# Two weight blocks multiplied by seven products in place of eight, with the weight sums on GpSimd

## The reference, cut to what matters

```python
for l in range(DEPTH):                    # second_block, two layers
    h = rmsnorm(x, norm_g[l])             # 256 x 1024
    p = h @ w_in[l]
    (c_q, c_kv, k_r, gate_a, fq, fk, fv, ff, gate_b,
     shift_cols, gate_c, merge_cols) = split_cols(p, IN_SIZES)
    o_a = mla_branch(..., gate_a, ...)    # attention, times silu(gate_a)
    o_b = fox_branch(..., gate_b, ...)    # attention with decay, times silu(gate_b)
    o_c = rwkv_branch(..., gate_c, ...)   # recurrence, times silu(gate_c)
    g_a, g_b, g_c = jnp.split(merge_cols, 3, axis=-1)
    merged = (jax.nn.sigmoid(g_a) * (o_a @ w_pa[l]) + jax.nn.sigmoid(g_b) * (o_b @ w_pb[l])
              + jax.nn.sigmoid(g_c) * (o_c @ w_pc[l]))
    x = x + merged @ w_out[l]
```

## Time and profile before

| | us |
|---|---|
| median of 3 runs | 2013.91 (2013.78 to 2015.64) |
| the profiled execution | 2013.13 |
| its span, first to last instruction | 2011.3 |
| TensorE busy in the span | 1642.2 |
| VectorE busy | 575.9 |
| ScalarE busy | 336.2 |
| GpSimd busy | 144.8 |
| fill products (L1662), 768 records | 188.1 |

### The profile page before, as it was taken

How to read it: one execution, slowest core, us unless ns; L and a number is a source line. 1 busy time by engine, 2 the same in 40 slices (tenths; PEclk the granted TensorE clock), 3 DMA queues, 4 the chain that set the end, 5 groups by cost and what they waited for, 6 DMA issues and landing times.

```text
span 2011.3 us, 25746 instructions
## 1 busy us (share of the span) xinstructions
PE 1642.2 (82%) x11426; PEld 940.9 (47%) x11426; DVE 575.9 (29%) x1055; ACT 336.2 (17%) x725; POOL 144.8 (7%) x137
## 2 busy tenths in 40 slices
PE   6988865655657998665657559999999999999999
PEld 3544221111214863111212118887668687775785
DVE  0546010000105652100100013542433625533435
ACT  1141100000000001000000001342332013433320
POOL 0000000000000001000000000211021302110213
PEclk8998888887877998787887888999999999999999
DMA  9998999999999979999999993321532342214330
GB/s 403 415 394 318 426 427 428 428 428 428 428 428 427 426 280 411 423 428 427 428 428 428 428 428 115 127 78 33 212 146 97 118 175 83 85 45 185 147 114 33
DMA packets 45741, 588.67 MB, mean 293 GB/s; under 512 B 5184, under 2 KB 5344, under 8 KB 9920
## 3 DMA queue, kind: packets, MB, share of 16 engines
q1 hardware_dynamic: 42624, 575.05, 69.2%
q0 software_dynamic: 2576, 10.54, 1.3%
q10 hardware_dynamic: 432, 1.44, 0.2%
HBM read 585.96 MB, written 1.06 MB: 292 GB/s over the span
## 4 chain that ended last, share of the span: by engine, by line
PE 57%; DMA 38%; DVE 3%; ACT 2%; issue 1%; SPq 0%; ACTq 0%; DVEq 0%
DMA arena<-in_experts 37%; PE ps L1281 17%; PE ps L1662 8%; PE ps L1549 5%; PE ps L1685 4%; PE ps L1681 4%; PE ps L1454 3%; PE ps L2032 2%; DMA ring<-in_stream 1%; PE ps L1783 1%; PE ps L2062 1%; PE ps L2105 1%; PE ps L1245 1%; PE ps L1770 1%; PE ps L1561 1%
## 5 line engine op out<-in xcount | busy, mean ns | idle before, releaser
L1549 PE MATMUL ps<-arena 128*32 128x512 f32 x1372 | 218.9, 763 | 137.7 <-DMA arena<-in_experts 136.1
L1549 PE MATMUL ps<-ring,arena 128*32 128x512 f32 x1312 | 207.8, 763 | 117.1 <-DMA ring<-in_experts 114.3
L1281 PE MATMUL ps<-arena,ring 128*128 128x256 f32 (+1 forms) x992 | 192.2, 357 | 2.5 <-ACT arena L773 2.5
L1662 PE MATMUL ps<-arena,ring 128*128 128x256 f32 x768 | 188.1, 389 | 0.2 <-issue 0.2
L1281 PEld LDWEIGHTS ps<-arena,ring 128*128 128x128 f32 x992 | 171.1, 195 | 23.1 <-ACT arena L773 3.1
L1549 PEld LDWEIGHTS ps<-arena 128*32 128x32 f32 x1372 | 44.8, 125 | 277.5 <-DMA arena<-in_experts 150.8
L1549 PEld LDWEIGHTS ps<-ring,arena 128*32 128x32 f32 x1312 | 41.5, 126 | 252.6 <-DMA ring<-in_experts 139.7
L1662 PEld LDWEIGHTS ps<-arena,ring 128*128 128x128 f32 x768 | 139.8, 190 | 29.8 <-issue 10.6
L2482 DVE TENSOR_TENSOR arena<-ps,gate 128x512 f32<-128x512 f32 x16 | 10.3, 686 | 306.2 <-PE ps L1549 306.2
L1681 PE MATMUL ps<-arena,ring 128*128 128x256 f32 x384 | 89.5, 382 | 0.0
L881 ACT ACTIVATE arena<-ps,modcol 128x128 f32<-128x128 f32 x32 | 14.6, 457 | 434.0 <-PE ps L1561 434.0
(11 more groups left out here) (426 smaller groups left out, 2046.8 us busy)
## 6 DMA issues: line engine op xcount, KB each, us to landing
arena<-in_experts SPq DMA_DIRECT2D x85, 2048.0 KB, 40.7
ring<-in_experts SPq DMA_DIRECT2D x82, 2048.0 KB, 40.9
ring<-in_stream SPq DMA_DIRECT2D x59, 2048.0 KB, 8.8
spare<-in_experts SPq DMA_DIRECT2D x21, 2048.0 KB, 40.6
arena<-in_stream SPq DMA_DIRECT2D x13, 2048.0 KB, 20.8
spare<-in_stream SPq DMA_DIRECT2D x3, 2048.0 KB, 19.1
ring<-in_stream SPq DMA_DIRECT2D x2, 1696.0 KB, 7.3
arena<-in_stream SPq DMA_DIRECT2D x2, 1024.0 KB, 26.5
```

What stands on the lines that cost most here:

```text
L1281: mm = M(dst, lhs(k), rhs(k), start=k == 0, stop=k == n - 1)
L1549: mm = M(bank(b + half)[32 * e:32 * e + 32], x[:, k, 32 * e:32 * e + 32], wk(e, half), start=k == 0, stop=k == KD - 1, tile_position=(0, 3 ...
L1662: mm = M(bank(fill_bank(n))[:, x * T:x * T + T], slot(key)[:, k, c:c + P], s2["ht"][:, k], start=k == 0, stop=k == KD - 1)
```

## The change: seven products for eight

Eight of the nine blocks are put together in pairs, so that a pair is a matrix of 1024 x 1024. It is cut into quarters b11, b12, b21, b22 and multiplied by the tokens, which are cut in halves of 128 tokens and of four tiles. Seven products of quarters (16 products of 128 x 128 weights by 128 tokens each) stand in place of eight. Sums of weight quarters are made in place, in the slots, by GpSimd; sums of tokens once per layer by VectorE; ScalarE copies partial results out of PSUM and VectorE adds them. Three pairs are the whole fill of the recurrence, the fourth stands in the attention. A step of the filler is now two products of half the width. The order of the weights in the stream changes: gate_b goes behind the merge blocks of gate a, and latent behind the first half of merge gate b.

In the diff `pair_out` is a function of ScalarE's program, `product` and the seven lines behind it are TensorE's, `pair_in` and `filled` VectorE's, `decays`, `pair_differences`, `pair_updates` and the last `second` GpSimd's. ScalarE's and VectorE's parts are called at fixed points of their programs, each when the fill up to that point holds the product that it needs.

```diff
-FILLS = {(0, 0): dict(FILL, open=6, down=0, lora=5, kk_sum=15, rk_sum=8, gn_sum=27),
-         (1, 0): dict(FILL, open=4, down=2, lora=11, kk_sum=14, rk_sum=8, gn_sum=22),
-         (0, 1): dict(FILL, open=0, down=0, lora=6, kk_sum=15, rk_sum=8, gn_sum=32)}
+FILLS = {(0, 0): dict(FILL, open=6, down=0, lora=5, kk_sum=15, rk_sum=8, gn_mean=7, gn_sum=14),
+         (1, 0): dict(FILL, open=4, down=2, lora=9, kk_sum=14, rk_sum=8, gn_sum=14),
+         (0, 1): dict(FILL, open=0, down=0, lora=6, kk_sum=15, rk_sum=8, gn_mean=6, gn_sum=16)}
-ATT_FILL = (6, 0) + (6, 5) * 6 + (6, 6) * 2
+ATT_FILL = (6, 0) + (5, 5) * 6 + (6, 5) * 2
+PAIRS = ((("gate_c",), ("gate_a",)), (("merge", 0, 0), ("merge", 0, 1)), (("gate_b",), ("merge", 1, 0)),
+         (("merge", 2, 0), ("merge", 2, 1)))
+WOVEN = 3
+PRODUCTS = 7
+PRODUCT = 8
+PAIR = PRODUCTS * PRODUCT
+PLAIN = 6
...
-        add(("in", layer, "gate_b"), rows(wi[:, G_B:G_B + HALF]))
...
         merge(0, 0)
         merge(0, 1)
+        add(("in", layer, "gate_b"), rows(wi[:, G_B:G_B + HALF]))
+        merge(1, 0)
         add(("in", layer, "latent"), rows(wi[:, C_Q:G_A]))
-        merge(1, 0)
...
+            def pair_out(l, n, i):
+                if i == 0:
+                    act.wait_ge(*Sp.at(l, n, 0))
+                    if n:
+                        act.wait_ge(*Sv.at(l, n - 1, "sum22"))
+                    A(part_e, bank(7), ACT.Copy).then_inc(*Sa.up(l, n, "e"))
+                if i == 1 and n and n < WOVEN:
+                    pair_last(l, n - 1)
+                if i == 2:
...
+                    A(part_u, bank(7), ACT.Copy).then_inc(*Sa.up(l, n, "u"))
+                if i == 3:
+                    act.wait_ge(*Sv.at(l, n, "sum11"))
+                    pair_gate_out(l, n, 0, 0)
+                if i == 4:
+                    act.wait_ge(*Sp.at(l, n, 4))
+                    act.wait_ge(*Sv.at(l, n, "sum11"))
+                    A(part_e, bank(7), ACT.Copy).then_inc(*Sa.up(l, n, "w"))
...
+                if p:
+                    filled_to(l, pair_ends(1, 4))
...
+                def product(i, b, weights, tokens, fresh):
+                    for tile in range(4):
+                        for k in range(4):
+                            mm = M(bank(b)[:, tile * P:(tile + 1) * P], weights[:, k, tile * P:(tile + 1) * P], tokens[:, k],
+                                   start=fresh and tile == 0 and k == 0, stop=tile == 3 and k == 3, skip_group_check=True)
+                            if tile == 3 and k == 3:
+                                if i < PRODUCTS - 1:
+                                    mm.then_inc(*Sp.up(l, n, i))
+                                else:
+                                    mm.then_inc(used, 3 if n == WOVEN - 1 else 2)
+                            if k % 2:
+                                yield
...
+                yield from product(0, x, b11, ht[:, 0:4, 0:P], True)
...
+                yield from product(1, y, b21, ht[:, 4:8, 0:P], True)
+                pe.wait_ge(*Sa.at(l, n, "e"))
+                pe.wait_ge(*S("token_dve").at(l, 3))
+                pe.wait_ge(*So.at(l, n, "t2"))
+                yield from product(2, x, part_sum, token_sums[:, 1], False)
+                pe.wait_ge(*Sv.at(l, n, "sum11"))
+                pe.wait_ge(*So.at(l, n, "t3"))
+                yield from product(3, y, b11, token_sums[:, 2], True)
+                pe.wait_ge(*Sa.at(l, n, "u"))
+                yield from product(4, x, b12, token_sums[:, 0], False)
+                pe.wait_ge(*Sa.at(l, n, "w"))
+                yield from product(5, x, b22, token_sums[:, 3], False)
+                pe.wait_ge(*Sv.at(l, n, "sum22"))
+                pe.wait_ge(*So.at(l, n, "t4"))
+                yield from product(6, y, b21, ht[:, 4:8, P:T], False)
...
+            def pair_in(l, n, i):
+                if i == 1:
+                    ve.wait_ge(*Sp.at(l, n, 1))
+                    ve.wait_ge(*Sa.at(l, n, "e"))
+                    V.tensor_tensor(pair_quarter(n, 0, 0), by_tile4(bank(6)), by_tile4(part_e), ALU.add).then_inc(*Sv.up(l, n, "sum11"))
+                if i == 4:
...
+                if i == 6:
...
...
                 V.scalar_tensor_tensor(out=rw["kmod"], in0=rw["kmod"], scalar=1.0, in1=k, op0=ALU.add, op1=ALU.mult
                                       ).then_inc(*Sv.up("kmod", *K))
+                filled(3)
...
             def decays(l):
                 for j in range(4):
+                    if j == 2:
+                        pair_differences(l, WOVEN)
+                        pair_updates(l, WOVEN)
                     if j >= 2:
                         po.wait_ge(*Sv.at("score", 1, l, 2 + j))
...
+            def pair_differences(l, n):
+                for key in pair_keys(l, n):
+                    po.wait_ge(*has_landed(key))
+                G.tensor_tensor(b12, b12, b11, ALU.subtract).then_inc(*So.up(l, n, "t1"))
+                po.wait_ge(*So.at(l, n, "t1"))
+                if n:
+                    po.wait_ge(*Sp.at(l, n - 1, 2))
+                    po.wait_ge(*So.at(l, n - 1, "t4"))
+                G.tensor_tensor(part_sum, b22, b12, ALU.subtract).then_inc(*So.up(l, n, "t2"))
+
+            def pair_updates(l, n):
+                po.wait_ge(*So.at(l, n, "t2"))
+                po.wait_ge(*Sp.at(l, n, 0))
+                G.tensor_tensor(b11, part_sum, b11, ALU.subtract).then_inc(*So.up(l, n, "t3"))
+                po.wait_ge(*Sp.at(l, n, 1))
+                G.tensor_tensor(b21, b21, part_sum, ALU.subtract).then_inc(*So.up(l, n, "t4"))
...
             def second(l):
+                pair_differences(l, 0)
+                pair_updates(l, 0)
                 for p in range(2):
...
+                    if p == 0:
+                        pair_differences(l, 1)
+                        pair_updates(l, 1)
+                        pair_differences(l, 2)
+                    else:
+                        pair_updates(l, 2)
```

More of the change, by code:

```diff
@@ L625, in merge_gate @@
             return tab2[:, n_second + i * 2 * T:n_second + (i + 1) * 2 * T].rearrange("p (j t) -> p j t", j=2)
-        def merge_done(l, b, i):
[L629 to L641, removed]
+        part_sum = spare[:, 0:2048].rearrange("p (k n) -> p k n", k=4)
@@ new lines, in two_block_program, with pair_keys, pair_blocks, pair_gate @@
+        part_e = spare[:, 2048:2560]
+        part_u = spare[:, 2560:3072]
+        token_sums = ln_t[:, :].rearrange("p (i k t) -> p i k t", i=4, k=4)
+        def pair_keys(l, n):
+            return tuple(("in", l) + part for part in PAIRS[n])
+        def pair_blocks(l, n):
+            first, second_ = (slot(key) for key in pair_keys(l, n))
+            return first[:, 0:4], second_[:, 0:4], first[:, 4:8], second_[:, 4:8]
+        def pair_gate(n, j):
+            part = PAIRS[n][j]
+            if part[0] == "gate_c":
+                return s2["oc"]
+            if part[0] == "gate_a":
+                return at2["oa"]
+            if part[0] == "gate_b":
+                return at2["ob"]
+            if part[1] == 0:
+                return gates_kept[:, 4 * part[2]:4 * part[2] + 4]
+            if part[1] == 2:
+                return merge_late[:, 4 * part[2]:4 * part[2] + 4]
+            return tab2[:, n_second:n_second + 4 * T].rearrange("p (j t) -> p j t", j=4)
@@ L953, in recurrence, with pair_last, filled_to @@
+            def pair_last(l, n):
+                act.wait_ge(*S("pair_dve").at(l, n, "sum21"))
+                pair_gate_out(l, n, 1, 0)
+            pair_seen = {}
+            def filled_to(l, units):
+                for n in range(WOVEN):
+                    for i in range(PRODUCTS):
+                        if pair_seen.get(l, 0) < pair_ends(n, i) <= units:
+                            pair_out(l, n, i)
+                pair_seen[l] = units
             def recurrence(l, p):
@@ L985, in recurrence @@
                 A(rw["eH"], rw["eH"], ACT.Exp).then_inc(*Sa.up("eH", *K))
-                for point in range(5):
-                    filled(point)
+                filled(4)
                 act.wait_ge(*Sv.at("inv0", *K))
@@ L1126, in woven @@
             def woven(l, step):
-                for n in range(woven_by(step - 1), woven_by(step)):
-                    weave_out(l, n)
+                before, now = woven_units(step - 1), woven_units(step)
+                for i in range(PRODUCTS):
+                    if before < pair_ends(WOVEN, i) <= now:
+                        pair_out(l, WOVEN, i)
+                for n in (PLAIN, PLAIN + 1):
+                    if before < weave_end(n) <= now:
+                        if n == PLAIN:
+                            pair_last(l, WOVEN)
+                        weave_out(l, n)
             def attention2(l):
@@ L1655, in fill_tiles, with weave_tiles @@
+            def fill_tiles(l):
+                for n in range(WOVEN):
+                    yield from pair_tiles(l, n)
+            def weave_tiles(l):
+                for n, (key, i, _) in enumerate(weave_jobs(l)):
```

(2 more changed lines are left out.)

148 lines of the change are left out of this document (115 added, 33 removed).

## The result

| | median us (lowest to highest) | ratio to the kernel before, 95% interval |
|---|---|---|
| before | 2013.85 (2013.27 to 2015.64, 4 runs) | |
| changed | 2092.64 (2090.36 to 2094.66, 4 runs) | 1.0395 [1.0383, 1.0408] |

The change makes the kernel 78.8 us slower; 2088 was forecast, within 2042 to 2110. The profiled execution of the changed kernel took 2090.36 us (span 2088.5).

A forecast was written before the change was run, and what follows sets the result against it. TensorE was taken as the bound, 99.77 of 100 us busy. The profiled 2013.13 us, +62.2 of lateness (savings inside) and +11.8 of clock gave 2087.1; 0.8 more for the median made 2088 us, range 2042 to 2110.

The forecast's parts named there:

- products saved: Filler in recurrence, norms and attention: fewer units at 0.43 us each, 13.7 us a layer, 27.5 us in both.
- waits: TensorE's lateness behind held VectorE operations, copies and fq's load, both layers: +62.2 us, the saved units inside.
- clock: Behind idles of over 5 us TensorE gets half clock: half of 23.6 us taken, 11.8; bounds 0 and 23.6.
- Rival (3): A 128-column product takes as long as a 256-column one: 2179 us; chance 0.02.
- A, B: First recurrence: GpSimd sums hold VectorE's token difference and scan; TensorE's next decay-stage sum comes 10.0 us late.
- C: Turn to second recurrence: sums hold VectorE's scaling and affine, +3.5 us; layer 1's state steps held, +4.0 more.
- D: Second recurrence: product five waits for ScalarE's copy of product four, 1.0 us.
- G: Before the first fq product: fq's load waits for pair 2's slot, +3.3 us, with 6.0 saved us lost.
- F: Attention: pair 3's four sums hold the scalings that TensorE's transposes wait for, +11.3 us, bounds +3 to +15.
- Rival (1): Attention: a head pair's four scalings pass in one turn, two sums less lost each: 2069 us; chance 0.2.
- Rival (2): Not slower: the GpSimd sums fall into VectorE's gaps: 2012 us; chance 0.07.

The follow-up runs named there:

- e1: The changed kernel with each GpSimd weight sum working on only 64 of its 2048 columns: 2022.99 us.
- e2: The changed kernel with pair 3, in the attention, by eight products in the old fill order: 2069.24 us.
- e3: The changed kernel with pair 2's products reordered so that fq's load is asked for earlier, ahead of ukv's: 2071.06 us.
- e4: The changed kernel with each GpSimd sum issued as eight instructions over 128x256 instead of one over 128x2048: 2059.68 us.
- e5: The changed kernel with the recurrence's sums moved, some onto VectorE, every pair's products reordered, fq's load early and pair 3 by eight products: 2018.80 us.

## Why the prediction was right

The mechanism is the one predicted, and e1 to e4 each came out within 2 us of the theory's number or inside its range. By its terms, against the account in the section on the result, both counted from the profiled 2013.13 us:

| term | predicted | measured |
|---|---|---|
| products saved | -27.5 | -20.4 |
| waits (TensorE's idle; the sum of 62.2 without the saving) | +89.7 | +75.3 |
| clock | +11.8 | +26.7 |
| block two | +74.0 | +81.6 |
| start of block two, and median for profiled run | +0.8 | -2.1 |

So the mechanism was foreseen, and that the time came within 5 us is partly luck: the saving was put 7.1 us too high, the waits 14.4 too high and the clock 14.9 too low, and these nearly cancel.

- **Products.** The new unit was put at the price of the old, 0.43 us. (The 30 records of the earlier trace rows are 15 units in 6.64 us, which is 0.44.) Inside the fill, where other products cut it into short groups, the old ones took 93.8 us for 192 units of layer 0's recurrences, 0.489 each, and e5's new ones 87.7 us for 168, 0.522 each or 0.13 a record, not the 0.107 that the prediction named. That the short groups are the reason is not tested. Rival (3), a product as long as one of twice its columns, is out, but the halves do cost more than half.
- **A, B.** 9.4 us in layer 0 against 10.0. The scan was held there as foreseen (4.94 us against 1.21); the token difference lost 1.8 us, not 3.1, because sums one and two ended 1.2 us earlier against it. In layer 1 they cost 13.5: there sums three and four came at other moments, the scan ran its 1.22 us, and an operation of 128x1024 (5.41 us) and two of 128x256 (4.80), which the prediction's sum had not counted, were held instead.
- **C.** From layer 0's first Gram products to the second recurrence's first sum: +4.4 us net of the units, +3.5 predicted. In layer 1 8.5 against 7.5, with the state step held as forecast (4.11 us for two operations that took 0.48 together).
- **D.** 0.7 us of wait (1.0), but 3.7 us of lateness: the clock behind C lies here.
- **G.** 9.2 us of wait, 9.3 predicted.
- **F.** Waits of 9.9 and 10.4 us, where 14.7 stands in the sum without the units; the four sums met the scalings of two steps, and the reductions between were not held. From the first fq product to the layer's last, the half clock behind G and F included, 14.1 us a layer were lost against 11.3, and e2 puts the choice as a whole at 11.7. Rival (1) falls: both steps' scalings took over 7 us.
- **Clock.** Half of the 23.6 was taken "since TensorE waits again soon". It lost 26.7, more than the upper bound of 23.6: there were twelve stretches at 0.50, not eight, as waits of 2.6 to 5 us were followed by them too. In e1 even an idle of 1.5 us in layer 0's state step was followed by 3.4 us at 0.50.

The rule of the Trainium skill, "SBUF — State Buffer", section "Who interferes with whom", goes further than the prediction used it: a VectorE instruction with one SBUF input that is not in a two-port mode does not contend with GpSimd. The trace agrees: the two reductions kept their 0.42 and 0.68 us under a sum, while scalings with one SBUF input, which the page lists among those that can enter such a mode, took 4.38 and 2.53 us, in place of 0.43 and 0.17. Which mode they ran in, no trace shows. So the prediction's "operations that read SBUF alone do not run" was too wide.

Rival (2), not slower, needed sums three and four of pair 0 done before the decay chain and those of pair 3 within one step of attention. In the changed kernel the first ran from 1264.25 us, under the decay scaling and the scan, and the others reached over two steps. e5 puts the sums elsewhere, six of a layer's twelve on VectorE, and leaves pair 3 out: nearly all of the loss goes, and by its trace the products' own waits eat the saving.

## What to carry to other kernels

Work given to an idle GpSimd is not free for VectorE: price each GpSimd instruction that reads SBUF at its full length for the first VectorE operation of SBUF data that meets it (reductions and reciprocals passed here), look up which operation that is and who waits for it, and cut the instruction small if it can't be moved. A scheme that saves products on a TensorE that is busy all the time has to keep every new dependence (copies between products, a block that comes free later) away from it; here each wait of 4.3 to 5.7 us cost another 1.7 to 3 in clock (half the busy time of the stretch at 0.50). Price a filler product in the company in which it runs, not in a long row.

## What the runs showed of the hardware

- VectorE and GpSimd take turns by instruction, both ways: eight GpSimd pieces of 128x256 take 5.5 us alone and up to 8.63 with VectorE's operations between; one of 128x2048 takes 4.5 to 5.2 us whatever waits.
- Reductions and reciprocals of SBUF data pass a GpSimd sum (0.42, 0.68, 0.18 us); scalings are held, down to 128x4 (2.53 us).
- At a granted clock of 0.50 TensorE's records take about twice as long (six in 5.36 us, against 2.74 at 1.00): with half of that time taken off, the busy time of the changed kernel and of e1 agree to 0.2 of 719 us.
- The sum of 128x2048 takes 4.5 us on GpSimd and 2.3 on VectorE.
